# Twelve conditioning rows move from TensorE in the attentions to VectorE in the gate stages

## The reference, cut to what matters

```python
silu_c, silu_cc = silu(c), silu(c_ctx)           # two streams: latent and context
for l in range(2):
    mod   = silu_c  @ w_ada[l] + b_ada[l]        # [1024] @ [1024, 6*1024]
    mod_c = silu_cc @ w_ada[l] + b_ada[l]
    sh1, sc1, g1, sh2, sc2, g2 = split(mod, 6)   # the same for mod_c
    h = rms_norm(x) * (1 + sc1) + sh1
    # mixer: q, k, v = h @ w_in; a global attention (8 heads), a window attention
    # (4 heads, with a sink), a Fourier mix; then the gated merge:
    g = sigmoid(h @ w_in[:, 1536:])              # 3 branches of 1024 columns
    m = g[0]*(f_mix @ w_br_fourier) + g[1]*(o_g @ w_br_global) + g[2]*(o_w @ w_br_window)
    x = x + g1 * (m @ w_out)
    x = x + g2 * experts(rms_norm(x) * (1 + sc2) + sh2)    # 16 experts, each takes its tokens
# the second block: six rows of its own, from w_mod_2 and c_2, a recurrent mixer, a SwiGLU
```

## Time and profile before

| what | value |
|---|---|
| median of three runs | 2308.28 us (2319.6, 2303.8, 2308.28) |
| span of the profiled execution | 2316.9 us, 21565 instructions |
| busy share of the span: TensorE, VectorE, ScalarE | 88%, 29%, 19% |
| chain that ended last | TensorE 70%, DMA 21%, VectorE 4%, ScalarE 2% |
| DMA | 598.15 MB, 258 GB/s over the span |
| L1286 (dense products) | 562.0 us busy |
| L1252 (the rows' products) | 576 records, 71.1 us busy |

### The profile page before, as it was taken

One profiled execution on the slowest core, in us unless ns is written; L12 is line 12 of the kernel. 1 busy time (PEld: TensorE's weight loads), 2 busy tenths in 40 slices (PEclk: granted clock), 3 DMA queues, 4 the chain that ended last, 5 costly groups with the idle time before them and its releaser, 6 DMA issues.

```text
span 2316.9 us, 21565 instructions
## 1 busy us (share of the span) xinstructions
PE 2036.9 (88%) x8606; PEld 1003.2 (43%) x8606; DVE 670.7 (29%) x1613; ACT 430.6 (19%) x884; POOL 0.2 (0%) x4
## 2 busy tenths in 40 slices
PE   6999899999988889888999978789776688979998
PEld 3445444444432323333554433333222255748863
DVE  2275311124211212124560132122211158730001
ACT  3045300014200000002151022103100032530000
POOL 0000000000000000000000000000000000000000
PEclk8999999999999989998999988999897899989999
DMA  9237722322599999996394548999999963132432
GB/s 366 76 145 304 270 82 64 101 90 109 216 421 422 430 428 429 429 427 243 127 345 137 191 199 330 425 420 422 431 427 429 429 237 109 37 109 102 153 136 82
DMA packets 111614, 598.15 MB, mean 258 GB/s; under 512 B 9255, under 2 KB 15223, under 8 KB 86811
## 3 DMA queue, kind: packets, MB, share of 16 engines
q1 hardware_dynamic: 107920, 591.82, 63.9%
q10 hardware_dynamic: 3595, 4.95, 0.6%
HBM read 595.71 MB, written 1.05 MB: 258 GB/s over the span
## 4 chain that ended last, share of the span: by engine, by line
PE 70%; DMA 21%; DVE 4%; ACT 2%; issue 2%; DVEq 0%; SPq 0%; ACTq 0%
PE bank L1286 24%; DMA weight_ring<-in_w_up_e 14%; PE bank L1696 8%; PE bank L638 7%; PE bank L1723 4%; PE bank L1679 4%; PE bank L657 3%; PE bank L1235 3%; PE bank L1252 3%; DMA weight_ring<-in_w_down_e 2%; DMA arena<-in_w_up_e 2%; PE bank L1522 2%; PE bank L435 2%; PE bank L1456 2%; DMA weight_ring<-in_w_ada 1%
## 5 line engine op out<-in xcount | busy, mean ns | idle before, releaser
L1286 PE MATMUL bank<-weight_ring,arena 128*128 128x512 f32 (+1 forms) x1328 | 562.0, 585 | 4.0 <-DMA weight_ring<-in_w_in 2.0
L1286 PEld LDWEIGHTS bank<-weight_ring,arena 128*128 128x128 f32 x1328 | 252.7, 191 | 308.8 <-issue 299.1
L1696 PE MATMUL bank<-weight_ring,arena 128*64 128x512 f32 x832 | 247.1, 642 | 55.3 <-DMA weight_ring<-in_w_up_e 43.2
L1679 PE MATMUL bank<-weight_ring,arena 128*32 128x512 f32 x816 | 152.5, 767 | 67.4 <-DMA weight_ring<-in_w_up_e 52.7
L1723 PE MATMUL bank<-weight_ring,arena 128*64 128x512 f32 (+1 forms) x800 | 179.1, 593 | 12.3 <-DMA weight_ring<-in_w_down_e 11.2
L1696 PEld LDWEIGHTS bank<-weight_ring,arena 128*64 128x64 f32 x832 | 80.0, 148 | 180.0 <-issue 179.7
L638 PE MATMUL bank<-arena,weight_ring 128*128 128x256 f32 x704 | 153.6, 381 | 0.8 <-DVE small L2339 0.8
L3100 ACT ACTIVATE arena<-bank 64x512 f32<-64x512 f32 (+1 forms) x64 | 37.7, 589 | 624.6 <-PE bank L1696 398.1
L638 PEld LDWEIGHTS bank<-arena,weight_ring 128*128 128x128 f32 x704 | 134.7, 191 | 19.7 <-issue 1.1
L1235 PE MATMUL bank<-const,arena 128*128 128x128 f32 (+3 forms) x764 | 106.1, 286 | 33.8 <-DVE arena L2504 6.4
L1235 PEld LDWEIGHTS bank<-const,arena 128*128 128x128 f32 (+3 forms) x764 | 90.5, 165 | 84.6 <-issue 64.2
(11 more groups left out here) (388 smaller groups left out, 1840.8 us busy)
## 6 DMA issues: line engine op xcount, KB each, us to landing
weight_ring<-in_w_up_e SPq DMA_DIRECT2D x52, 2048.0 KB, 14.3
weight_ring<-in_w_gate_e SPq DMA_DIRECT2D x51, 2048.0 KB, 16.1
weight_ring<-in_w_down_e SPq DMA_DIRECT2D x50, 2048.0 KB, 13.1
weight_ring<-in_w_in SPq DMA_DIRECT2D x25, 2048.0 KB, 10.0
weight_ring<-in_w_ada SPq DMA_DIRECT2D x24, 2048.0 KB, 12.3
arena<-in_w_down_e SPq DMA_DIRECT2D x14, 2048.0 KB, 15.8
arena<-in_w_gate_e SPq DMA_DIRECT2D x13, 2048.0 KB, 16.4
arena<-in_w_up_e SPq DMA_DIRECT2D x12, 2048.0 KB, 17.3
```

The costliest lines, as they stand in the source:

```text
L1286: mm = pe.matmul(b[:, 0:c1 - c0], lhs[:, k, t * P:t * P + P], slot_view(r)[:, k, c0:c1], start=(k == 0), stop=(k == ks - 1))
L1679: mm = pe.matmul(b[c:c + R, :], xgT[1][:, KH * half + k, e, :], wide(r)[:, k, n * 512:n * 512 + 512], start=(half == 0 and k == 0), stop=( ...
L1696: mm = pe.matmul(banks_[n][c:c + R, :], xgT[l][:, KH * half + k, e, 0:R], wide(r)[:, k, n * 512:n * 512 + 512], start=(half == 0 and k == ...
```

## The change

Twelve rows leave the attentions: (1,0) to (1,5) and (2,0), (2,1), which stood in layer 0's, are now made in layer 0's gate stage, and the four others of l = 2 in layer 1's. The rows of l = 0 stay where they are, and so do the steps -1 to 2 of layer 0. In layer 1's attention no row is left.

A moved row is summed by VectorE: for each of the 8 blocks of 128 weight rows it multiplies a block of [128, 1024] with a column of silu(c) and adds it to a running sum (`sum_rows`). Rows with seg 0 and 1 do it for two streams, the others for one. TensorE adds over the partitions, with a column of ones (`reduce_rows`): for shift and scale rows the running sum is the stationary, in eight pieces of 128 columns, and the result already lies along the partitions; for gate rows the ones are the stationary and the sum moves, 2 products of 512 columns. VectorE adds the bias (`take_rows`). The weights come in pieces of two blocks, 1 MB, into two buffers in the arena, from SP's queue (`load_row_pieces`): a piece waits until the piece before the last is used, the first until attention is over. `SUMMED` says which rows are summed before which branch's gate products. The sum stands in VectorE's order before the products of branch i, the reduction in TensorE's before the gates of branch i + 1.

```diff
-    first = {-1: ((0, 2), None), 0: ((0, 3), None), 1: ((0, 4), (0, 3)), 2: ((0, 5), (0, 4)), 4: ((1, 0), None), 5: ((1, 1), (1, 0)),
-             6: ((1, 2), (1, 1)), 7: ((1, 3), None), 8: ((1, 4), (1, 3)), 9: ((1, 5), None), 10: (None, (1, 4))}
-    second = {-1: ((2, 0), None), 0: ((2, 1), (2, 0)), 1: ((2, 2), (2, 1)), 2: ((2, 3), None), 3: ((2, 4), (2, 3)), 4: ((2, 5), (2, 4))}
-    return early, {0: first, 1: second}
+    first = {-1: ((0, 2), None), 0: ((0, 3), None), 1: ((0, 4), (0, 3)), 2: ((0, 5), (0, 4))}
+    return early, {0: first, 1: {}}
+
+def summed_rows():
+    first = [[(1, 0)], [(1, 1), (1, 2)], [(1, 3), (1, 4)], [(2, 0)], [(2, 1), (1, 5)], []]
+    second = [[(2, 2)], [(2, 3)], [(2, 4)], [(2, 5)], [], []]
+    return {0: first, 1: second}
+
+def row_streams(seg):
+    return 2 if seg < 2 else 1
...
+        mod_piece = [area(at, 2, D) for at in (8192, 17408)]
+        mod_acc = (area(12288, 2, D), area(14336, 1, D))
...
+            def reduce_rows(rows_):
+                for i, (l, seg) in enumerate(rows_):
+                    acc = mod_acc[i]
+                    pe.wait_ge(S("row_summed"), due("row_summed"))
+                    b = bank("D")
+                    if seg % 3 == 2:
+                        for n in range(2):
+                            mm = pe.matmul(b[32 * n:32 * n + 32, :], ones.to_broadcast([P, 32]), acc[:, 0, n * 512:n * 512 + 512],
+                                           start=True, stop=True)
+                    else:
+                        by_row = l < DEPTH and seg > 2
+                        for s in range(row_streams(seg)):
+                            for k in range(KD):
+                                cols_ = every8(k) if by_row else slice(k * P, k * P + P)
+                                mm = pe.matmul(b[:, 2 * k + s:2 * k + s + 1], acc[:, s, cols_], ones, start=True, stop=True)
+                    mm.then_inc(S("fullD"), 1)
...
                 for n in range(2):
                     for br, ks in ((0, 2), (1, 4), (2, 2)):
+                        if n or br:
+                            reduce_rows(SUMMED[l][3 * n + br - 1])
                         rg = next_slot()
...
+                def load_row_pieces(rows_):
+                    for lr, seg in rows_:
+                        src = LAYERS[lr]["w_mod"][:, seg * D:seg * D + D].rearrange("(h k p) n -> h p k n", h=4, p=P)
+                        for h in range(4):
+                            n = due("mod_pieces")
+                            if n > 2:
+                                sp.wait_ge(S("mod_piece_used"), n - 2)
+                            sp.dma_start(mod_piece[n % 2], src[h]).then_inc(S(f"mod_piece_landed{n % 2}"), 16)
+
+                load_branch(0, 0)
+                load_branch(0, 1)
+                sp.wait_ge(S("fullA"), heads_out_jobs[l])
+                for i in range(6):
+                    load_row_pieces(SUMMED[l][i])
+                    if i < 4:
+                        load_branch((i + 2) // 3, (i + 2) % 3)
+                    else:
+                        load_cols(A["w_out"][l], 512 * (i - 4), 512 * (i - 4) + 512)
...
+            def sum_rows(rows_):
+                for i, (l, seg) in enumerate(rows_):
+                    acc, streams = mod_acc[i], row_streams(seg)
+                    for h in range(4):
+                        piece = due("mod_pieces") % 2
+                        dve.wait_ge(S(f"mod_piece_landed{piece}"), due(f"mod_piece_landed{piece}", 16))
+                        for j in range(2):
+                            for s in range(streams):
+                                k = 2 * h + j
+                                signal = "mod_piece_used" if j and s == streams - 1 else "dve_step"
+                                c = silu_c[:, l, k, s:s + 1]
+                                if k:
+                                    dve.scalar_tensor_tensor(out=acc[:, s, :], in0=mod_piece[piece][:, j, :], scalar=c, in1=acc[:, s, :],
+                                                             op0=ALU.mult, op1=ALU.add).then_inc(S(signal), 1)
+                                else:
+                                    dve.tensor_scalar(acc[:, s, :], mod_piece[piece][:, j, :], c, None, ALU.mult).then_inc(S(signal), 1)
+                                dve.wait_ge(S(signal), due(signal))
+                    dve.memset(flag, 0.0).then_inc(S("row_summed"), 1)
...
                 dve.wait_ge(S("shift_sums_ready"), due("shift_sums_ready"))
+                sum_rows(SUMMED[l][0])
...
                 for n in range(2):
                     for br in range(3):
+                        if n or br:
+                            take_rows(SUMMED[l][3 * n + br - 1])
+                            sum_rows(SUMMED[l][3 * n + br])
                         for t in own:
```

46 lines of the change are left out of this document (35 added, 11 removed).

## The result

The changed kernel takes 2341.6 us (median of 4 runs, 2333.0 to 2343.0), against 2313.9 for the kernel before in the same runs: a ratio of 1.011, interval 1.008 to 1.014. It is 1.1% slower, outside the predicted range.

A forecast was written before the change was run, and what follows sets the result against it. Gate stages were taken as TensorE's own time, attention without rows as bound by ScalarE's chain. 20 + 12 - 26.0 - 1.3 = 4.7 us gained, 2308.3 to 2303.6, say 2304; range 2297 to 2311 (50%).

The forecast's parts named there:

- Attention, 20 and 12 us: Attention of layers 0 and 1: taking rows out gains 20 and 12 us, with the chain through ScalarE remaining.
- the step without a row: Layer 0's attention, step 3: no conditioning row, yet value products start 9.2 us apart, with TensorE last released by ScalarE.
- The third rival: Attention: shorter steps keep TensorE's clock low, so 8.7 us are lost, 2317 us; chance 16%.
- the first rival: Attention is TensorE's own time, so 36 + 25.5 us come out, 34 us gained net, 2274 us; chance 7%.
- I take 0.117 ... 26.0 us: Gate stages: reductions at 0.117 us a record plus 3.6 for gate rows, 26.0 us, between 15.7 and 43.5.
- The fourth rival: Gate stages: one-column products cost 0.191 us a record, 17.5 us lost against the forecast, 2321 us; chance 8%.
- Nothing hides them: Gate stages: these are TensorE's own time, so the 26.0 us of added reductions are paid in full.
- The last is late by 1.3: Layer 1's gate stage: the last of four rows' sums is done at 20.4 us against 19.1, 1.3 us counted.
- the second rival: Gate stages: at 7 us a piece sums come late and TensorE waits, 20 us lost, 2328 us; chance 16%.
- first landing 6.5 us after that end: Layer 0's gate stage, sum of (1,1) with (1,2): its first piece lands 6.5 us after the previous branch ends.
- its signs of being wrong: Profile after: pieces landing later than 6 us, long waits for sums, records far from 0.117, value products at half speed throughout.
- What VectorE gets, hidden: Gate stages: VectorE's running sums, 115 us in layer 0 and 38 in layer 1, fit under them if fed in time.

The follow-up runs named there:

- no_sums: The changed kernel with one multiplication per stream instead of each running sum and no row pieces loaded: 2330.0 us, 1.0064 to the kernel before.
- no_sums_even: As no_sums, but rows (1,3) and (1,4) are reduced from adjoining columns instead of every eighth: 1.0036 to the kernel before.
- no_reduce: The changed kernel without TensorE's reductions and without taking them, VectorE still summing all twelve rows: 2289.8 us, 0.9888 to the kernel before.
- no_rows: The changed kernel with moved rows not made at all (no sums, pieces or reductions; bias only): 2287.1 us, 0.9886 to the kernel before.
- unstride: The changed kernel with VectorE summing (1,3) and (1,4) in turned column order, so TensorE loads adjoining columns: 2343.7 us, 1.0129 to the kernel before.
- wide: The changed kernel with each small product of a reduction over 32 equal columns of ones instead of one: 2337.1 us, 1.0097 to the kernel before.
- wide_early: As wide, with SP also issuing the next sum's first two pieces ahead of the branch weights: 1.0061 to the kernel before.
- gate_rows_only: Against the kernel before, only the four gate rows (1,2), (1,5), (2,2), (2,5) leave attention and are summed on VectorE: 2305.6 us, 0.9950.

## Why the prediction was wrong

**Attention, 20 and 12 us: right.** It gave 19.3 and 9.7. What remains is the chain through ScalarE that the step without a row had shown. TensorE's timeline of the changed kernel, narrow steps of layer 0 and wide ones of layer 1:

```profile
231.39 1.08 PE L1648 MATMUL bank<-arena 128*64 128x256 f32 x8 [1.60 <-ACT arena L2863]
...
1203.52 3.00 PE L1648 MATMUL bank<-arena 128*64 128x256 f32 x16 [2.63 <-ACT arena L2863]
...
1213.20 3.68 PE L1648 MATMUL bank<-arena 128*64 128x256 f32 x16 [4.22 <-ACT arena L2863]
```

A narrow step takes 5.4 to 5.9 us, forecast 5.2, a wide one 8.4 to 9.7, forecast 8.3. The third rival, a clock that stays low in attention, is seen in single products (3.00 and 3.68 instead of 1.95, 2.8 us together), about what layer 1 fell short by (2.3). Attention as TensorE's own time, the first rival, is out.

**The price of the reductions, "I take 0.117 ... 26.0 us": right for adjoining columns, wrong for two rows.** A record measured 0.110 (3.52 us for 32 at 286.01) and a gate row 0.98, forecast 0.9. But (1,3) and (1,4) have every eighth column as stationary, 0.23 a record, above even the upper bound of 0.191. The reductions are 24.5 us in layer 0, as measured (1.1 of it is low clock behind the wait at 463.51), and 5.4 in layer 1 at full clock, as in no_sums: 29.9, 3.9 over the forecast, and no_sums_even shows that the stride is the reason. The fourth rival was right in kind for two rows of twelve.

**"Nothing hides them", and nothing counted behind them: the step that failed first.** The sum took the dense products behind a reduction at the 34.2 and 41.1 us of the earlier trace rows. The low clock made them 6.3 us longer in layer 0, nearly all of it behind runs of small products with TensorE never idle; the prediction had looked for a low clock only in attention and behind waits. The kernel before could have told it. In layer 0's attention, where TensorE had not been idle since 157.82, its timeline has

```profile
176.14 2.08 PE L1265 MATMUL bank<-const,gate_rows 34*64 34x2 f32 x32
178.16 3.45 PE L1235 MATMUL bank<-const,arena 128*128 128x128 f32 x16
```

a run of 32 small records, and behind it 16 turnings that take 3.45 us instead of 1.97. It doesn't happen behind every such run: at 254.28, behind the next one of this form in layer 0's narrow steps, eight turnings take their usual 1.09.

**"The last is late by 1.3": the step that failed second.** The waits are 7.7 us: 1.4, 3.3 and 3.0. The refill was sized rightly (5.3 against 5.2), and 7 us a refill, the condition of the second rival, didn't come; its waits did, for another reason. What failed is the line "first landing 6.5 us after that end": the first piece shares the engines with 2 MB of gate weights and the branch weights that SP issued ahead of it, and landed 9.2 and 15.6 us after the end of the branch in layer 1, where a sum has no slack. In layer 0 the 1.4 us are those of (2,1) with (1,5), a load as long as the one that the prediction found hidden with 2.5 us to spare. Each wait also brought the low clock, 6.8 us together with the reductions that ran in it. This 13.1 in layer 1 is what no_sums takes away.

Together: reductions 29.9, waits 7.7, low clock 13.6 (6.3, 6.8 and 0.5 that I can't place in layer 1), 51.2 us, against 27.3. With attention 3.0 short and 1.9 elsewhere, this is the 28.8 us between the forecast change of the span and the measured one. The largest part, the 13.6 us of low clock in the gate stages, stood in no rival. Of its signs of being wrong three came: pieces that land later than 6 us after their issue, long waits for the sums, and records far from 0.117 (those of two rows).

**What VectorE gets, hidden: right as long as nobody waits for a sum.** no_reduce against no_rows shows no cost of 115 and 38 us of sums on VectorE; what they cost is their lateness, above.

**Open.** Which reductions have a low clock behind them isn't settled. It fell behind 3.6 us reductions with one column and with 32, behind those of 1.8 us only in some cases where TensorE had waited just before them (in unstride a wait of 0.22 us, 1.95 us of reduction, then 19.11 us of dense products instead of 17.41), and the same reduction had it in wide and not in wide_early. That a chain of better-fed one-column reductions in layer 1 could reach zero waits wasn't shown; each of three ways of feeding moved the waits.

## What to carry to other kernels

Moving work off TensorE is paid for by what TensorE must still do for it: price the part that stays, and the dense products behind it, before the part that goes. When filler is taken from in front of another engine's chain, the gain of each further piece shrinks once the chain is what comes last (layer 1's attention here); take out those that are cheap to bring back, as gate_rows_only did, and stop. A transfer issued behind big weights shares the engines with them, whichever queue it is in, so for a sum with little slack count all the bytes on their way, and not its own alone. Sending the first two pieces ahead only moved the wait to the third; that all of them ahead would do it was not tried. Before crediting a small kernel change with a shorter stage, compare a stretch that it leaves alone: here one of 48 us differed by 4.9 between executions.

## What the runs showed of the hardware

- A run of 3.6 us of small products that kept TensorE busy without a gap (3.60 of 3.60 us, granted clock 0.98) was followed by 3.4 us of dense products at 0.52. Three of layer 0's five reductions had it behind them, and it cost some 1.9 to 2.5 us each time (branches of 36.1, 36.7 and 43.0 us from start to start, against 34.2 and 41.1 before). The Trainium skill (TensorE: Matmul & The Clock Gate, HAM oscillation) tells of a clock that falls in the waits between short bursts of products; here there was no wait ahead of the fall, so that rule doesn't cover it.
- A product with a 128x128 stationary of every eighth column and one moving column takes 0.23 us a record instead of 0.11, at either level of the clock, also with 32 moving columns (7.58 us for 32 records in wide). The Trainium skill (SBUF — State Buffer, Door 1: The DMA port swizzle) says that each access that crosses to a new 16-byte line pays a penalty; every eighth column is a new line each time. The traces agree in kind, for TensorE's stationary and, below, for VectorE; that the lines are the reason no run here shows. The prediction had not weighed it.
- 32 moving columns cost the same as one: 3.65 and 3.63 us for 32 records.
- VectorE's multiply-add on 128x1024 takes 2.1 us when its input is read at every eighth column (the sums are read and written in adjoining order), 1.285 otherwise; the plain multiplication takes 1.15 instead of 0.75.
